# Order of the two gather streams of an expert mixer: V rows ahead of U rows in each pair, with small moves in opening, selection and end

## The chip, the cores and the metric

The kernel runs on one NeuronCore of a Trainium2 chip. The metric is device time in microseconds (us) of one execution. Engines are called by their short names: PE is TensorE, ACT is ScalarE, DVE is VectorE, POOL is GpSimd, SP is SyncE.

## The reference, cut to what matters

One layer of a decoder is computed for 256 prompt tokens and 8 sample tokens of width 2048. The first half (projections, gated linear attention, short convolution, output projection) is dense matmul work and takes the first 940 us. The second half is an expert mixer, and the change is mostly there:

```
ht = h.reshape(T, D)
q = (ht @ w_query).reshape(T, PEER_HEADS, 2, DQ_HALF)       # 8 heads, 2 halves
s1, s2 = scores of both halves against 128 keys each
v1, i1 = lax.top_k(s1, 16);  v2, i2 = lax.top_k(s2, 16)
top, pos = lax.top_k(v1[..., :, None] + v2[..., None, :], 16)   # of 256 candidates
idx = i1 * 128 + i2 at pos;  g = softmax(top)
u = expert_u[idx];  a = einsum('thkd,td->thk', u, xb)      # dot of each U row with the token
w = g * gelu(a)
y = x + einsum('thk,thkd->td', w, expert_v[idx])           # weighted sum of V rows
y = rmsnorm(y, norm_f_g)
```

For each token and head 16 rows of 8 KB are read from `expert_u`, and the same 16 from `expert_v`. The weight of a V row is known only when all 16 dots of that head and token are done.

## The kernel before, in words

**Blocks.** The 256 prompt tokens are two tiles of 128. A block `b` is one head of one tile: blocks 0 to 7 are the 8 heads of tile 0, blocks 8 to 15 those of tile 1. A block needs 16 gathers (`s` = 0 to 15) from `expert_u` and 16 from `expert_v`; one gather is one indirect DMA of POOL (L736) that brings 128 rows of 8 KB (1 MB) into one slot of a ring. The sample tokens add 8 U gathers in block 10 and 8 V gathers in block 12.

**U and V.** The U gathers of block `b` lie beside the V gathers of block `b-1`: the loop over `b` and `s` issues U(b, s) and then V(b-1, s). The U row set is consumed by DVE: `dot` (L1513) multiplies it with the tokens and sums. After the last dot of a block ACT applies Gelu (L1065), DVE scales with the softmax share and spreads the result (L1553, L1528), PE turns it (L1951), and DVE makes `weigher` of it (`turned_w`, L1546). DVE's program has `weights_of(b-1)` after dot(b, 0) and `turned_w(b-1)` after dot(b, 1). Only then PE may consume V(b-1, 0): `weigh` (L1970), 4 matmuls a gather that accumulate in a PSUM bank. In blocks 1 and 9 a `begin_sum` (L1958, 4 matmuls) goes ahead of the first `weigh` of each four.

**The ring.** `order_of` is the list of all gathers in order; gather n takes slot n % 6 up to n = 35 and then slot (n - 36) % 8. `free_slot` lets POOL wait until the gather that had the slot before is eaten: by DVE's count `u_used` or PE's count `pe_used`. POOL issues strictly in the order of the list, so one slot that isn't free holds up every gather behind it. Block 1 begins with gather 16, on a ring of 6; from its middle on the ring has 8.

**Beside it.** DVE also finds the experts of block b+1 during block b: `keys_of` after dot(b, 1), `pairs_of` after dot(b, 4), `experts_of` after dot(b, 7). PE makes the query projections of the heads 3 to 7 in blocks 1 to 3. SP loads `w_query` in pieces of 2 MB while the gathers run, and when the last query matmul is done (L581) it loads `gf_c`, the final norm's factors, spread over the partitions (L583).

**Opening.** The 256 prompt tokens are scaled with 1/rms in eight pieces of 512 columns: two by DVE (L1138), three by ACT (L795), three by POOL (L658). PE turns 16 column blocks (`turn(k)`, L1725), ACT and DVE split each into two parts (`act_hi` L799, `act_lo` L1148), and the small projection `rank_rows(g)` (L1738) is put between turns: g = 0 after turn 11, g = 1 after turn 14, g = 2 and 3 after all. Then `first_queries` (L1749) begins the dense part.

**Selection.** For block 0 the experts are found in two halves of eight (`first_experts`, L1443), so that the first gathers can go before the second half is known. POOL's first gather waits for the count `retrieved` (L1473).

**End.** Tile 1's outputs go out in four parts: ACT squares a bank (L1026), PE sums over partitions (L1996), DVE makes the mean (L1567), ACT the root (L1033), DVE the reciprocal (L1576) and the scaled result times `gf_c` (L1579), and SP stores it with four DMAs (L593).

## Time and profile before

| what | value |
|---|---|
| median of 3 runs (lowest, highest) | 2303.8 us (2303.49, 2305.24) |
| time of the profiled execution | 2304.25 us |
| its span | 2302.5 us |
| PE, DVE, ACT, POOL busy | 1586.5, 1318.1, 559.9, 731.2 us |
| DMA moved | 780.93 MB, mean 339 GB/s |
| of it by POOL's queue (the gathers) | 597.80 MB |
| issue to landing, median, U and V gathers | 17.0 and 17.3 us |

The table has averages over two very different halves. Up to about 940 us PE is busy nine tenths and more; after that the DMA engines are busy nine tenths and more. So a row of the whole span says little, and each stage has to be read for itself. The executions agree within 0.08%.

### The profile page before, as it was taken

How to read it: one execution, taken by the hardware profiler on the slowest of the kernel's cores; microseconds unless marked ns; L12 is line 12 of the kernel's file. 1: busy time of each engine (PE TensorE's matmuls, PEld its weight loads, DVE VectorE, ACT ScalarE, POOL GpSimd, SP SyncE). 2: the span in 40 equal slices, each digit the busy share in tenths (PEclk: the TensorE clock that was granted, in tenths of full speed). 3: DMA queues.
4: the chain of work that ended last, by engine and by line, in shares of the span. 5: the costliest groups of instructions: out<-in, count | busy, mean ns of one | idle time of the engine just before them, and what ended most of it. 6: DMA issues, size and time to landing. Idle time of an engine off the chain costs nothing.

```text
span 2302.5 us, 26069 instructions
## 1 busy us (share of the span) xinstructions
PE 1586.5 (69%) x10425; PEld 1088.1 (47%) x10425; DVE 1318.1 (57%) x2002; ACT 559.9 (24%) x775; POOL 731.2 (32%) x735
## 2 busy tenths in 40 slices
PE   9999999999999999957674334444343334434345
PEld 8999999999999999834341000000000000000001
DVE  6544556646555564675554665566566665465541
ACT  5333555545555544310000000000000000000000
POOL 1000110110111101444553444544345554344342
PEclk9999999999999999988885555555565555555556
DMA  8876878887878776799999999999999999999998
GB/s 243 224 192 197 237 227 240 247 247 211 256 209 252 220 227 211 292 417 427 423 427 392 388 427 427 427 428 427 427 422 427 427 427 427 428 427 423 427 414 349
DMA packets 435165, 780.93 MB, mean 339 GB/s; under 512 B 39640, under 2 KB 353904, under 8 KB 367200
## 3 DMA queue, kind: packets, MB, share of 16 engines
q0 software_dynamic: 89424, 597.80, 62.6%
q1 hardware_dynamic: 344000, 179.19, 28.1%
q10 hardware_dynamic: 1624, 2.31, 0.3%
q8 instruction: 82, 1.34, 0.2%
q14 instruction: 35, 0.29, 0.0%
HBM read 755.95 MB, written 23.35 MB: 338 GB/s over the span
## 4 chain that ended last, share of the span: by engine, by line
PE 45%; DMA 39%; DVE 6%; POOL 6%; issue 4%; ACT 1%; POOLq 0%; ACTq 0%; DVEq 0%
DMA ring<-in_expert_u,idx_all 27%; PE bank L1770 12%; PE bank L1771 12%; PE bank L1772 12%; DMA ring<-in_expert_v,idx_turned 10%; POOL ring L736 6%; DVE ring L1513 3%; PE bank L1970 3%; PE bank L1924 2%; DMA ring<-in_expert_v,idx_s 1%; DMA ring<-in_expert_u,idx_s 1%; PE bank L1880 1%; PE bank L1861 1%; DMA x2T<-x_turned 0%; DVE weigher L1546 0%
## 5 line engine op out<-in xcount | busy, mean ns | idle before, releaser
L1970 PE MATMUL bank<-ring,weigher 128*32 128x512 f32 x2048 | 450.1, 976 | 624.8 <-DMA ring<-in_expert_v,idx_turned 567.3
L1513 DVE CUSTOM_DVE_ANT_0 ring<-ring,xn_tok 128x2048 f32<-128x2048 f32 x256 | 585.8, 2291 | 477.0 <-DMA ring<-in_expert_u,idx_all 475.9
L1770 PE MATMUL bank<-act_hi,w_hi 128*128 128x264 f32 x2272 | 653.0, 287 | 0.3 <-DVE x2T L1369 0.3
L1771 PE MATMUL bank<-act_lo,w_hi 128*128 128x264 f32 x2272 | 643.8, 283 | 0.0
L1772 PE MATMUL bank<-act_hi,w_lo 128*128 128x264 f32 x2272 | 643.5, 283 | 0.0
L1110 DVE TENSOR_TENSOR w_lo<-raw,w_hi 128x2048 fp32r<-128x2048 f32 x142 | 325.6, 2293 | 321.3 <-ACT w_hi L771 320.6
L1970 PEld LDWEIGHTS bank<-ring,weigher 128*32 128x32 f32 x2048 | 53.0, 136 | 952.5 <-DMA ring<-in_expert_v,idx_turned 867.8
L736 POOL DMA_INDIRECT ring<-in_expert_u,idx_all x256 | 301.3, 1177 | 431.7 <-DVE w_all L1513 274.4
L1770 PEld LDWEIGHTS bank<-act_hi,w_hi 128*128 128x128 f32 x2272 | 427.9, 188 | 19.5 <-issue 19.1
L1771 PEld LDWEIGHTS bank<-act_lo,w_hi 128*128 128x128 f32 x2272 | 428.2, 188 | 1.7 <-issue 1.7
L1772 PEld LDWEIGHTS bank<-act_hi,w_lo 128*128 128x128 f32 x2272 | 426.0, 187 | 0.0
L736 POOL DMA_INDIRECT ring<-in_expert_v,idx_turned x256 | 305.1, 1192 | 324.4 <-PE bank L1970 257.5
L771 ACT ACTIVATE w_hi<-raw 128x2048 fp32r<-128x2048 f32 x142 | 272.1, 1916 | 417.3 <-PE bank L1772 413.4
L690 POOL DMA_DIRECT2D out<-s_ring x64 | 34.9, 545 | 496.6 <-DVE s_ring L1325 496.6
L1065 ACT ACTIVATE w_all<-w_all 128x16 f32<-128x16 f32 x16 | 3.5, 216 | 659.1 <-DVE w_all L1513 659.1
L1924 PE MATMUL bank<-h2T,wq 128*128 128x264 f32 x448 | 119.7, 429 | 0.0
L1924 PEld LDWEIGHTS bank<-h2T,wq 128*128 128x128 f32 x448 | 93.5, 213 | 38.2 <-issue 20.8
L1017 ACT ACTIVATE soft<-soft,rstd 128x16 f32<-128x16 f32 x16 | 4.9, 307 | 331.4 <-DVE soft L1418 331.3
L1951 PEld LDWEIGHTS bank<-div,widened 128*128 128x128 f32 x64 | 15.1, 293 | 110.3 <-issue 93.7
L1951 PE MATMUL bank<-div,widened 128*128 128x16 f32 x64 | 17.9, 359 | 63.7 <-DVE widened L1528 63.3
L664 POOL DMA_DIRECT2D v_samples<-v_tok x1 | 0.8, 754 | 163.4 <-DVE v_tok L1233 163.4
L998 ACT ACTIVATE q_s<-bank 128x8 f32<-128x8 f32 x16 | 2.8, 173 | 134.6 <-PE bank L1924 134.1
(318 smaller groups left out, 1183.2 us busy)
## 6 DMA issues: line engine op xcount, KB each, us to landing
raw<-in_w_in SPq DMA_DIRECT2D x129, 1024.0 KB, 6.8
s_ring<-in_state_gla POOLq DMA_DIRECT2D x64, 256.0 KB, 6.0
out<-s_ring POOLq DMA_DIRECT2D x64, 256.0 KB, 5.8
raw<-in_w_out SPq DMA_DIRECT2D x16, 1024.0 KB, 5.5
wq<-in_w_query SPq DMA_DIRECT2D x8, 2048.0 KB, 20.8
v_row<-v_samples POOLq DMA_DIRECT2D x32, 256.0 KB, 6.0
ring<-in_expert_u,idx_all POOLq DMA_INDIRECT x256, 17.0
ring<-in_expert_v,idx_turned POOLq DMA_INDIRECT x256, 17.3
```

Of the source, the lines that this page charges most:

```text
L690: g.dma_start(st_out[:, step // M, k, j, :], s_ring[step % N_S][:]).then_inc(s_out[step % N_S], 16)
L736: g.indirect_dma_start(ring[slot_of[n]][:], None, table, bass.IndirectOffsetOnAxis(ap=idx, axis=0)).then_inc(ring_in[slot_of[n]], 16)
L771: a.activation(w_hi[n0 % 2][:], raw[s][:], ACT.Copy).then_inc(hi_done, 1)
L1110: v.tensor_tensor(w_lo[n0 % 2][:], raw[s][:], w_hi[n0 % 2][:].bitcast(F32), ALU.subtract).then_inc(lo_done, 1)
L1513: v.tensor_tensor_reduce(ring[k][:], ring[k][:], xn_tok[:, b // PH, :], 1.0, 0.0, ALU.mult, ALU.add, w_all[:, b * TOPK + s:b * TOPK + s + ...
L1770: mm(out, hi_, act_hi[:, k, :], start=(k == 0), stop=False)
L1771: mm(out, hi_, act_lo[:, k, :], start=False, stop=False)
L1772: ins = mm(out, lo_, act_hi[:, k, :], start=False, stop=(k == KT - 1))
L1861: ins = mm(bank[KV0 + k][:], k_tok[:, k, :], v_, start=True, stop=True)
L1924: ins = mm(out, w[:, k, cols_], h2T[:, k, :], start=(k == 0), stop=(k == KT - 1))
L1951: mm(bank[z_bank(kind, b)][:, 0:TOPK], widened[n % 2][:].rearrange("p j k -> p (j k)"), div8[:], start=True, stop=True).then_inc(z_mm, 1)
L1970: ins = mm(bank[sum_bank(t, j)][c * STRIP:(c + 1) * STRIP, :], weigher[b % 2][:, s, :], ring[k][:, c * 512:(c + 1) * 512], start=False, st ...
```

## The change

It does five things.

1. `order_of` and POOL's loop: in each pair V(b-1, s) now comes ahead of U(b, s). The slots follow the list. POOL's wait for `retrieved` moves with the U gather. DVE's and PE's programs keep their order; only the slots that they name change.
2. Opening: the piece (part 3, tile 1) is scaled by DVE and no longer by ACT; `rank_rows(0)` goes after turn 13, `rank_rows(1)` after the last turn.
3. Selection of block 0: `match_replace` of the 256 candidates goes from ahead of the first `retrieved` to behind it; the cast of the first half's keys goes up between the two key searches.
4. End: for the last quarter of tile 1 the product with `gf_c` is made ahead of the mean, the scaling is split into 256 columns on DVE and 256 on ACT, and of the four stores SP issues two and ACT two.
5. Four matmuls of the identity (`warm`) go ahead of PE's wait for the last V gather.

```diff
@@ -62,6 +62,7 @@
     B_END = B_QRY + 2 * PH
     N_PAR = 6
     WARM = (16, 16, 4)
+    LAST_WARM = 4
     STRIP = 32
     N_CONSTS, N_LATE_CONSTS = 25, 12
     N_LINKS = 18
@@ -279,6 +280,7 @@
         ROWS = 4
         QUERIES = {1: (3, 4), 2: (5, 6), 3: (7,)}
 
+        LEFT, RIGHT = (slice(3 * 512 + x * 256, 3 * 512 + (x + 1) * 256) for x in range(2))
         TILE_0, SAMPLES = [(0, j) for j in range(4)], [(2, 0)]
         Y_ORDER = TILE_0 + SAMPLES + [(1, j) for j in range(4)]
 
@@ -296,10 +298,10 @@
         order_of = []
         for g in range(N_BLK + 1):
             for s in range(TOPK):
+                if g > 0:
+                    order_of.append((V_, g - 1, s, "pe"))
                 if g < N_BLK:
                     order_of.append((U_, g, s, "dot"))
-                if g > 0:
-                    order_of.append((V_, g - 1, s, "pe"))
                 if g == S_U and s % 2:
                     order_of.append((US_, 0, s // 2, "dot"))
                 if g == S_V and s % 2:
@@ -585,9 +587,9 @@
             yp = y_prompt.rearrange("b l d -> (b l) d")
             ys = y_sample.rearrange("b s d -> (b s) d")
             for nth, (t, j) in enumerate(Y_ORDER):
-                sp.wait_ge(y_ready, nth + 1)
+                sp.wait_ge(y_ready, nth + 1 if nth < N_SUM - 1 else N_SUM + 2)
                 rows = TS if t == 2 else STRIP
-                for c in range(4):
+                for c in range(4 if nth < N_SUM - 1 else 2):
                     row0 = 0 if t == 2 else t * P + j * STRIP
                     out = (ys if t == 2 else yp)[row0:row0 + rows, c * 512:(c + 1) * 512]
                     sp.dma_start(out, y_out_at[c * STRIP:c * STRIP + rows, t, j * 512:(j + 1) * 512]).then_inc(y_out, 16)
@@ -737,19 +739,21 @@
                                      bass.IndirectOffsetOnAxis(ap=idx, axis=0)).then_inc(ring_in[slot_of[n]], 16)
 
             for b in range(N_BLK + 1):
-                if b < N_BLK:
-                    pool.wait_ge(retrieved, b + 2 if b else 1)
                 if b == S_U:
                     pool.wait_ge(s_picked, 1)
                 for s in range(TOPK):
+                    if b > 0 and s == 0:
+                        pool.wait_ge(z_read, nth_z("idx", b - 1) + 1)
+                    if b > 0:
+                        fetch(ev, V_, b - 1, s, idx_turned[:, (b - 1) % 3, s:s + 1])
+                    if b == 0 and s == 0:
+                        pool.wait_ge(retrieved, 1)
                     if b == 0 and s == 8:
                         pool.wait_ge(retrieved, 2)
-                    if b == 1 and s == 0 or b > 1 and s == 0:
-                        pool.wait_ge(z_read, nth_z("idx", b - 1) + 1)
+                    if 0 < b < N_BLK and s == 0:
+                        pool.wait_ge(retrieved, b + 2)
                     if b < N_BLK:
                         fetch(eu, U_, b, s, idx_all[:, b * TOPK + s:b * TOPK + s + 1])
-                    if b > 0:
-                        fetch(ev, V_, b - 1, s, idx_turned[:, (b - 1) % 3, s:s + 1])
                     if b == S_U and s % 2:
                         fetch(eu, US_, 0, s // 2, idx_s[:, s // 2:s // 2 + 1])
                     if b == S_V and s % 2:
@@ -790,8 +794,8 @@
             act.wait_ge(par_T, 1)
             a.activation(pcol[:], bank[0][:, 0:120], ACT.Copy).then_inc(par_ready, 1)
             act.wait_ge(rs_done, 1)
-            for part, t in ((1, 0), (1, 1), (3, 1)):
-                cols_ = slice(part * 512, (part + 1) * 512)
+            for t in range(2):
+                cols_ = slice(512, 1024)
                 a.activation(x_tok[:, t, cols_], x_tok[:, t, cols_], ACT.Copy, scale=rstd[:, t:t + 1]).then_inc(xa_done, 1)
             act.wait_ge(par_ready, 1)
             for k in range(KT):
@@ -1091,6 +1095,13 @@
             for j in range(4):
                 y_squares([(1, j)])
                 y_roots(2 + j, [(1, j)])
+            act.wait_ge(y_ready, N_SUM)
+            act.wait_ge(y_rstd, 6)
+            a.activation(y_out_at[:, 1, RIGHT], y_out_at[:, 1, RIGHT], ACT.Copy, scale=y_rs[:, N_SUM - 1:N_SUM]).then_inc(y_ready, 1)
+            act.wait_ge(y_ready, N_SUM + 2)
+            for c in (2, 3):
+                act.dma_start(y_prompt.rearrange("b l d -> (b l) d")[P + 3 * STRIP:2 * P, c * 512:(c + 1) * 512],
+                              y_out_at[c * STRIP:(c + 1) * STRIP, 1, 3 * 512:4 * 512]).then_inc(y_out, 16)
 
 
 
@@ -1138,6 +1149,8 @@
                     v.tensor_scalar(x_tok[:, t, cols_], x_tok[:, t, cols_], rstd[:, t:t + 1], None,
                                     ALU.mult).then_inc(xn_done, 1)
                 v.tensor_scalar(xs_n[:], xs_flat[:], rstd[:, 2:3], None, ALU.mult).then_inc(xs_scaled, 1)
+                cols_ = slice(3 * 512, 4 * 512)
+                v.tensor_scalar(x_tok[:, 1, cols_], x_tok[:, 1, cols_], rstd[:, 1:2], None, ALU.mult).then_inc(xn_done, 1)
 
             def act_parts():
 
@@ -1407,6 +1420,8 @@
                     work = [(sc[:, 0, 0, s, :], val[:, s, :], key_u[:, s, :])]
                     top8(work, 0)
                     top8(work, 1)
+                    if s == 0:
+                        v.tensor_copy(key_f[:, 0, :], key_u[:, 0, :])
 
             def best_pairs(r, rows):
                 chained(v.tensor_tensor(cand[r, :].rearrange("p (a b) -> p a b", a=TOPK),
@@ -1443,8 +1458,7 @@
             def first_experts():
 
                 shape = [P, TS, TOPK]
-                for s in range(2):
-                    v.tensor_copy(key_f[:, s, :], key_u[:, s, :])
+                v.tensor_copy(key_f[:, 1, :], key_u[:, 1, :])
                 chained(v.tensor_tensor(cand[:].rearrange("p (a b) -> p a b", a=TOPK),
                                         val[:, 0, :].unsqueeze(2).broadcast_to([P, TOPK, TOPK]),
                                         val[:, 1, :].unsqueeze(1).broadcast_to([P, TOPK, TOPK]), ALU.add))
@@ -1452,8 +1466,6 @@
                     eight = slice(8 * turn, 8 * turn + 8)
                     chained(v.max(best[:, eight], cand[:]))
                     chained(v.max_index(pos[:, eight], best[:, eight], cand[:]))
-                    if turn == 0:
-                        v.match_replace(cand[:], best[:, eight], cand[:], NEG_BIG)
                     v.tensor_scalar(pos_u[:, 0, eight], pos[:, eight], 4, None, ALU.logical_shift_right)
                     chained(v.tensor_scalar(pos_u[:, 1, eight], pos[:, eight], 15, None, ALU.bitwise_and))
                     for s in range(2):
@@ -1472,6 +1484,8 @@
                     chained(ins)
                     v.scalar_tensor_tensor(out=idx_all[:, eight], in0=key_sel[:, 0, eight], scalar=float(NKEY),
                                            in1=key_sel[:, 1, eight], op0=ALU.mult, op1=ALU.add).then_inc(retrieved, 1)
+                    if turn == 0:
+                        chained(v.match_replace(cand[:], best[:, eight], cand[:], NEG_BIG))
                 v.tensor_tensor(soft[:], best[:], best[:, 0:1].broadcast_to([P, TOPK]), ALU.subtract).then_inc(soft_in, 1)
                 chained(v.scalar_tensor_tensor(out=idx_f[:], in0=key_sel[:, 0, :], scalar=float(NKEY),
                                                in1=key_sel[:, 1, :], op0=ALU.mult, op1=ALU.add))
@@ -1696,9 +1710,18 @@
                                 y_means(nth, parts)
                             if s == 6:
                                 y_scale(nth, parts)
-            for j in range(4):
+            for j in range(3):
                 y_means(2 + j, [(1, j)])
                 y_scale(2 + j, [(1, j)])
+            dve.wait_ge(y_ss, N_SUM)
+            v.tensor_tensor(y_out_at[:, 1, 3 * 512:4 * 512], bank[sum_bank(1, 3)][:], gf_c[:], ALU.mult).then_inc(y_ready, 1)
+            y_means(5, [(1, 3)])
+            dve.wait_ge(y_root, 6)
+            v.reciprocal(y_rs[:, N_SUM - 1:N_SUM], y_rt[:, N_SUM - 1:N_SUM]).then_inc(y_rstd, 1)
+            dve.wait_ge(y_rstd, 6)
+            dve.wait_ge(y_ready, N_SUM)
+            v.tensor_scalar(y_out_at[:, 1, LEFT], y_out_at[:, 1, LEFT], y_rs[:, N_SUM - 1:N_SUM], None,
+                            ALU.mult).then_inc(y_ready, 1)
 
 
 
@@ -1718,7 +1741,7 @@
                 if k == 8:
                     pe.wait_ge(xp_done, 2)
                 if k == 12:
-                    pe.wait_ge(xa_done, 3)
+                    pe.wait_ge(xn_done, 3)
                     pe.wait_ge(xp_done, 3)
                 b = bank[2 + k % 6]
                 for t in range(2):
@@ -1799,10 +1822,9 @@
                 if k == 2:
                     pe.wait_ge(xs_scaled, 1)
                     tr(bank[1][:, 2 * P:3 * P], xs_n[:], ident[:]).then_inc(xs_tr, 1)
-                if k == 11:
+                if k == 13:
                     rank_rows(0)
-                if k == 14:
-                    rank_rows(1)
+            rank_rows(1)
             rank_rows(2)
             rank_rows(3)
             pe.wait_ge(par_ready, 1)
@@ -1965,6 +1987,8 @@
                     pe.wait_ge(z_read, nth_z("w", b) + 1)
                 if b % PH == 0 and s % 4 == 0:
                     begin_sum(t, j)
+                if b == N_BLK - 1 and s == TOPK - 1:
+                    warm(LAST_WARM)
                 pe.wait_ge(ring_in[k], landed(V_, b, s))
                 for c in range(4):
                     ins = mm(bank[sum_bank(t, j)][c * STRIP:(c + 1) * STRIP, :], weigher[b % 2][:, s, :],
```

The order of the instructions shows what moves. POOL, the gathers from number 16 on (first pair of block 1; `ring_194` to `ring_199` are the six slots), before:

```order
L736 DMA ring_198<-in_expert_u,idx_all 128x2048 [waits u_used,z_read,retrieved]
L736 DMA ring_199<-in_expert_v,idx_turned 128x2048 [waits u_used]
L736 DMA ring_194<-in_expert_u,idx_all 128x2048 [waits u_used]
L736 DMA ring_195<-in_expert_v,idx_turned 128x2048 [waits u_used]
L736 DMA ring_196<-in_expert_u,idx_all 128x2048 [waits u_used]
L736 DMA ring_197<-in_expert_v,idx_turned 128x2048 [waits u_used]
L736 DMA ring_198<-in_expert_u,idx_all 128x2048 [waits u_used]
L736 DMA ring_199<-in_expert_v,idx_turned 128x2048 [waits pe_used]
```

and with the change:

```order
L738 DMA ring_198<-in_expert_v,idx_turned 128x2048 [waits u_used,z_read]
L738 DMA ring_199<-in_expert_u,idx_all 128x2048 [waits u_used,retrieved]
L738 DMA ring_194<-in_expert_v,idx_turned 128x2048 [waits u_used]
L738 DMA ring_195<-in_expert_u,idx_all 128x2048 [waits u_used]
L738 DMA ring_196<-in_expert_v,idx_turned 128x2048 [waits u_used]
L738 DMA ring_197<-in_expert_u,idx_all 128x2048 [waits u_used]
L738 DMA ring_198<-in_expert_v,idx_turned 128x2048 [waits pe_used]
L738 DMA ring_199<-in_expert_u,idx_all 128x2048 [waits u_used]
```

The first wait for PE (`pe_used`) comes one gather earlier, at gather 22 and not at 23, and a U gather now stands behind it.

PE in the opening, from turn 11 on (L1725 are turns, L1738 `rank_rows`), before:

```order
L1738 MATMUL bank<-act_hi,raw_69 32x264 [waits xs_lo,raw_in0,par_ready,al_done]
L1738 MATMUL bank<-act_hi,raw_69 32x264 x3
L1738 MATMUL bank<-act_lo,raw_69 32x264 x4
L1725 MATMUL bank<-ident,x_tok 128x128 [waits xp_done,xa_done,al_done]
L1725 MATMUL bank<-ident,x_tok 128x128
```

and with the change (L1748 are turns, L1761 `rank_rows`):

```order
L1748 MATMUL bank<-ident,x_tok 128x128 [waits xp_done,xn_done,al_done]
L1748 MATMUL bank<-ident,x_tok 128x128
L1748 MATMUL bank<-ident,x_tok 128x128 [waits al_done]
L1748 MATMUL bank<-ident,x_tok 128x128
L1761 MATMUL bank<-act_hi,raw_69 32x264 [waits xs_lo,raw_in0,par_ready,al_done]
```

The turns 12 and 13 stand ahead of the first `rank_rows`, and turn 12 waits for DVE's piece in place of ACT's.

## Rows read from the trace of the kernel before

**Rows 1.** The page's GB/s line: 40 equal slices of 57.6 us.
```profile
GB/s 243 224 192 197 237 227 240 247 247 211 256 209 252 220 227 211 292 417 427 423 427 392 388 427 427 427 428 427 427 422 427 427 427 427 428 427 423 427 414 349
```
**Rows 2.** Busy time by stretch; the last three columns are clock, DMA share, GB/s.
```profile
1220.00:1240.00 20.00, 6.34 (x26) 1.10 (x26) 8.10 (x7) 0.00 (x0) 7.51 (x9) 0.55 1.01 382
...
1300.00:1320.00 20.00, 8.28 (x34) 1.31 (x34) 13.58 (x27) 0.00 (x0) 10.76 (x8) 0.50 1.01 387
...
1340.00:1360.00 20.00, 8.09 (x34) 1.50 (x34) 12.86 (x27) 1.50 (x2) 7.82 (x7) 0.50 1.01 426
```
**Rows 3.** Timeline of SP at 1200 to 1230: start, us, engine, line, operation.
```profile
1214.58 1.74 SPq L583 DMA_DIRECT2D gf_c<-in_norm_f_g  x4
```
**Rows 4.** Timeline, beginning of block 5: [idle before <- what ended it].
```profile
1344.79 2.29 DVE L1513 CUSTOM_DVE_ANT_0 ring<-ring,xn_tok 128x2048 f32<-128x2048 f32 x1 [2.56 <-DMA ring<-in_expert_u,idx_all]
...
1349.74 2.29 DVE L1513 CUSTOM_DVE_ANT_0 ring<-ring,xn_tok 128x2048 f32<-128x2048 f32 x1 [2.24 <-DMA ring<-in_expert_u,idx_all]
...
1351.96 0.69 DVE L1546 TENSOR_TENSOR weigher<-bank,own 128x512 f32<-128x512 f32 x1
...
1352.70 3.64 PE L1970 MATMUL bank<-ring,weigher 128*32 128x512 f32 x16 [4.48 <-DVE weigher L1546]
1354.94 0.94 POOL L736 DMA_INDIRECT ring<-in_expert_v,idx_turned  x1 [6.63 <-PE bank L1970]
```
**Rows 5.** DMA issues at 950.5 to 951.5: the first gather, us from issue to landing.
```profile
ring<-in_expert_u,idx_all POOLq DMA_INDIRECT x1, 5.7
```
**Rows 6.** Timeline, beginning of block 1.
```profile
1013.78 0.94 POOL L736 DMA_INDIRECT ring<-in_expert_u,idx_all  x1 [0.31 <-issue]
1014.28 2.29 DVE L1513 CUSTOM_DVE_ANT_0 ring<-ring,xn_tok 128x2048 f32<-128x2048 f32 x1 [1.11 <-DMA ring<-in_expert_u,idx_all]
...
1017.24 1.94 PE L1958 MATMUL bank<-x_tok,ident 128*32 128x512 f32 x8 [3.34 <-DVE weigher L1546]
...
1021.00 2.29 DVE L1513 CUSTOM_DVE_ANT_0 ring<-ring,xn_tok 128x2048 f32<-128x2048 f32 x1 [0.94 <-DMA ring<-in_expert_u,idx_all]
1021.17 2.93 POOL L736 DMA_INDIRECT ring<-in_expert_v,idx_turned  x1 [6.45 <-PE bank L1970]
...
1030.61 1.07 PE L1970 MATMUL bank<-ring,weigher 128*32 128x512 f32 x8 [0.38 <-DMA ring<-in_expert_v,idx_turned]
```
**Rows 7.** Timeline: dot(9, 0), V(8, 4)'s issue; then dot(15, 0), V(14, 4)'s issue.
```profile
1661.05 2.29 DVE L1513 CUSTOM_DVE_ANT_0 ring<-ring,xn_tok 128x2048 f32<-128x2048 f32 x1 [2.59 <-DMA ring<-in_expert_u,idx_all]
...
1672.96 2.10 POOL L736 DMA_INDIRECT ring<-in_expert_v,idx_turned  x1 [8.38 <-PE bank L1970]
...
2178.46 2.29 DVE L1513 CUSTOM_DVE_ANT_0 ring<-ring,xn_tok 128x2048 f32<-128x2048 f32 x1 [2.57 <-DMA ring<-in_expert_u,idx_all]
...
2188.56 2.80 POOL L736 DMA_INDIRECT ring<-in_expert_v,idx_turned  x1 [6.57 <-PE bank L1970]
```
**Rows 8.** Timeline of the opening.
```profile
11.73 1.32 DVE L1138 TENSOR_SCALAR x_tok<-x_tok,rstd 128x512 f32<-128x512 f32 x2
...
12.19 1.94 ACT L795 ACTIVATE x_tok<-x_tok,rstd 128x512 f32<-128x512 f32 x3
...
20.21 1.21 ACT L799 ACTIVATE act_hi<-bank,pcol 128x256 fp32r<-128x256 f32 x3 [1.21 <-PE bank L1725]
...
24.13 0.40 PE L1749 MATMUL bank<-act_hi,w_hi 128*128 128x264 f32 x1
```
**Rows 9.** Timeline of DVE, selection of block 0.
```profile
947.83 0.09 DVE L1456 MATCH_VALUE_LOAD cand<-best,cand 128x8 f32 x1
947.91 0.41 DVE L1456 MATCH_REPLACE8 cand<-best,cand 128x256 f32<-128x256 f32 x1
```
**Rows 10.** Timeline of the end; then line L593: min, median, max in ns.
```profile
2297.69 0.16 DVE L1567 TENSOR_SCALAR y_ms<-bank 128x1 f32<-128x1 f32 x1 [3.46 <-PE bank L1996]
...
2298.32 0.75 DVE L1579 SCALAR_TENSOR_TENSOR x_tok<-bank,y_rs,gf_c 128x512 f32<-128x512 f32 x1
...
L593 SPq DMA_DIRECT2D out<-x_tok x36: 287/421/555, 1694.6 to 2300.4; - x36
```

## The prediction

> **What bounds the kernel now.** I read the page's slices first. From the eighteenth on, that is from about 980 us to 2290, the DMA engines move 417 to 428 GB/s in nearly every slice [rows 1]. A gather is 1,048,576 bytes, at 427 GB/s 2.45 us, and a pair 4.9. So the second half is a stream of gathers that runs without a hole, and DVE and PE follow it: the idle time ahead of dots and of V matmuls ends with a landing [rows 4]. Two slices stand out, 392 and 388. The table of stretches shows them as 100 us, from 1220 to 1320, in which five stretches of 20 us read 382 to 388 at a DMA share of 1.01; at 1340 it is 426 at the same share [rows 2]. The engines are as busy there, but slower. That stretch costs 100 x (1 - 386/427) = 9.6 us. No wait explains it. It begins within some us of SP's loads of `gf_c` at 1214.58 [rows 3]. All four executions known lie within 1.8 us of each other, so each of them had it.
>
> Hence an exchange of U and V in a stream that is always full gains nothing by itself. It can lose, by a hole, and it can change that stretch.
>
> **Part 1, the pairs: the beginning of a block.** Call A the landing of V(b-1, 0). Nothing may eat it until dot(b, 1) is done and `weigher` is made. In block 5 dot(5, 0) starts at 1344.79, with its landing; dot(5, 1) at 1349.74, `weigher` at 1351.96, PE at 1352.70, and POOL issues V(4, 4), which needs the slot of V(4, 0), at 1354.94: 10.15 us behind dot(5, 0) [rows 4]. Before, V(4, 0) lands behind U(5, 0), now 2.45 us ahead of it. So POOL's issue comes at A + 10.15 + 2.45 = A + 12.6. Eight slots hold the stream until A + 8 x 2.45 = A + 19.6, when V(b-1, 4) must have landed. The trace has one gather with an empty queue, the first: 5.7 us from issue to landing [rows 5]. A + 12.6 + 5.7 = A + 18.3: 1.3 us early. The blocks 2 to 8 and 10 to 14 (twelve) therefore cost nothing; the cover is those 1.3 us. In the steady part V and U alternate as before, and nothing changes.
>
> The Trainium skill (DMA: Bandwidth & Descriptors, Anatomy of one DMA) fits a POOL-issued DMA as about 2.0 us plus bytes over 436 GB/s, which would be 4.4 us for a gather; the row says 5.7, and the row decides. By the page each of the three costs below would be smaller by 1.3 us, or zero, and the sum 2.9 us lower; I name it because it speaks for an easier change than I count.
>
> Three blocks have less cover.
> - Block 1, ring of six. Before, gather 22 is U(1, 3) and goes at 1013.78; V(0, 3) waits for PE until 1021.17 [rows 6]. Now gather 22 is V(0, 3). U(1, 1) is gather 19 and no longer 18; as 18 landed at 1014.28 and 20 at 1021.00, 19 is put in the middle, 1017.6, 3.4 us later. `weigher`, `begin_sum` at 1017.24 and the freed slot shift with it: POOL issues at 1021.17 + 3.4 = 1024.6, it lands at 1030.3, gather 23 at 1032.7. Before, 23 was eaten from 1030.61 on [rows 6]. Cost +2.1 us. Bounds: 0, as SP's `w_query` load can fill the hole, and +3.4, the full shift of the release, if nothing of it is absorbed.
> - Block 9, where `begin_sum` goes ahead. POOL's issue is 11.91 us behind dot(9, 0) and takes 2.10 us in place of 0.94, since it falls into a dot [rows 7]. Landing A + 2.45 + 11.91 + 5.7 + 1.16 = A + 21.2, so +1.6 us; bounds 0 and 2.45 (a whole gather).
> - Block 15: 10.10 us behind the dot, and 2.80 us long [rows 7]. Landing A + 12.55 + 5.7 + 1.86 = A + 20.1: +0.5 us; same bounds.
>
> At the end of the stream U(15, 15) lands one gather later and V(15, 0) is weighed some 2.5 us later; PE needs 3.64 us for two [rows 4] where the stream needs 4.9, so it catches up within a few gathers. Nothing.
>
> **Part 2, opening.** ACT's three pieces take 1.94 us [rows 8], 0.65 each; one goes to DVE, where two take 1.32 and DVE would otherwise wait for ACT. ACT starts its split 0.65 us earlier, and the 1.21 us that it stands still at 20.21, behind `rank_rows(0)` [rows 8], shrinks. But PE then has three `rank_rows` in a row to do, so I take only the first, -0.65, by which `first_queries` leaves 24.13 [rows 8]; the dense part is PE's and carries it on. Bounds 0 and -1.9 (both).
>
> **Part 3, selection.** `match_replace`, 0.09 and 0.41 with overlap [rows 9], leaves the way to the first gather. -0.5 at most, 0 at least. I take 0: the stream starts earlier, but block 1's hole is timed by DVE and PE and gives it back.
>
> **Part 4, end.** The scaling of 0.75 us becomes two halves beside each other, about 0.4 by DVE's pieces [rows 8], but the product of 0.75 is on DVE when the mean would start at 2297.69 [rows 10], which delays it by 0.3. Together 0. Two of SP's four stores, 0.42 us each [rows 10], go to ACT: -0.85. Bounds 0 and -1.2. The skill says (same page, Issuing engines are not separate DMA queues) that a second issuing engine saves only the issue time; that is just what I count. The four `warm` matmuls lie in PE's wait for a landing: 0, hidden by the stream.
>
> **Sum.** 2.1 + 1.6 + 0.5 - 0.65 + 0 - 0.85 = +2.7 us on the profiled execution's 2304.25, so 2306.9, and 2306.4 on the scale of the median, which lies 0.45 lower. What a measurement can tell from no change is 0.2%, 4.6 us. The small terms alone stay within it. What decides is the slow stretch.
>
> **Forecast: the slow stretch is gone, or nearly.** Its cost of 9.6 us leaves: 2306.4 - 9.6 = 2296.8, rounded 2297. For it: nothing in the program asks for this stretch; the 40 slices show it once in 1300 us, though loads, stores and block starts come many times; and the change gives the gathers another order and another distance to everything beside them just where it begins. Against it: I have no mechanism, only a coincidence in time, and `gf_c` is loaded at the same place of the program. Chance 0.40.
>
> **Rival 1: the stretch stays as it is,** because the load, or the end of the query matmuls beside it, makes it. Then the sum stands, 2306, which is no change. For it: four executions with the same time, so it is no accident. Chance 0.37.
>
> **Rival 2: the ring runs dry at every block start, slower.** The place is POOL's issue of V(b-1, 4), the cover 1.3 us. An issue that falls into a dot takes up to 2.80 us [rows 7], 1.86 more than usual. If that happens in the twelve blocks too, each lands at A + 12.6 + 5.7 + 1.86 = A + 20.2 and costs 0.55 us, together 6.6, and with the stretch in place the time is 2313. It decides as soon as issue and delay together pass A + 13.9. Against it: in block 5 the issue takes 0.94 [rows 4], as DVE is then at its small key operations and starts the next dot only behind them. A slow stretch that begins as before and lasts half as long again (+4.8, 2311) ends on the same side; both have 0.23. That the change doesn't do what it says is excluded by the order of the instructions.
>
> **How the numbers follow.** Faster by over 0.2%: 0.41 (the forecast, and a little of a stretch that is shortened). Within 0.2%: 0.36. Slower: 0.23. The range goes from 2292 (forecast with block 1, 9 and 15 at 0 and the opening at its better bound) to 2313 (rival 2). The forecast's own range is 2292 to 2300.
>
> **What would show it.** Slices of 427 GB/s where 392 and 388 stood: forecast; 387 from some point behind L585 on: rival 1. The wait of POOL for PE at block starts 2.45 us longer, 9.1 where 6.63 stood. A gap between dots of block 1 of 2 us more. The first `first_queries` matmul at 23.5. Two stores by ACT, and the time from the last V landing to the end 0.85 us shorter. DMA shares below 1.0 in a 20 us stretch at the start of blocks 2 to 14 would be rival 2. The forecast is wrong if the stretches of 387 together are longer than 50 us.

## The result, and the profile after

The changed kernel takes 2307.19 us (median of 20 executions, 2303.2 to 2337.1), the kernel before 2296.09 in the same comparison (20 executions, 2293.99 to 2305.74). The ratio is 1.0053 with a 95% interval of 1.0037 to 1.0069: slower by about half a per cent. The forecast was 2297, faster. It is wrong, in sign and in size.

The spread must be read with the medians. The kernel before has two groups of times: 12 of the 20 lie from 2294.0 to 2297.8, and 8 from 2303.5 to 2305.7. The three times known ahead of the prediction and the profiled execution (2304.25) belonged to the upper group. At its share in all executions of that kernel (36 of 125, below) four of four would come by pure chance about 7 times in a thousand, so why they did is open. Of the changed kernel, 8 of 20 lie from 2303.2 to 2304.3, and the others are spread up to 2337. So there are two questions: why the lowest times are 8 to 9 us apart, and what makes the long ones. The profiled execution after took 2328.71 us (span 2327.0) and shows both. Its slices, to be held against [rows 1]:

```profile
PEclk9999999999999999978885555555555555555556
DMA  9877877887878776899999999999999999999998
GB/s 251 224 191 200 241 228 237 245 236 222 240 230 255 209 225 220 328 379 426 423 412 376 377 376 410 424 421 419 428 402 427 428 424 427 427 425 423 428 412 351
```

Before, from the eighteenth slice on nearly all read 422 to 428, but for one dip. Now 376 and 377 stand in three slices in a row, and others read 379, 412, 410 and 402. The table of stretches (the last three columns are clock, DMA share and GB/s) shows the first kind:

```profile
1220.00:1240.00 20.00, 6.92 (x34) 1.27 (x34) 11.29 (x26) 0.00 (x0) 7.81 (x8) 0.56 1.02 373
1240.00:1320.00 80.00, 26.93 (x118) 3.70 (x114) 42.77 (x77) 3.09 (x4) 39.71 (x29) 0.52 1.01 377
1320.00:1400.00 80.00, 26.88 (x116) 4.15 (x116) 45.33 (x61) 3.09 (x4) 40.74 (x29) 0.52 1.01 376
...
1415.00:1420.00 5.00, 1.94 (x8) 0.20 (x8) 2.20 (x3) 0.00 (x0) 1.42 (x3) 0.50 1.03 415
1420.00:1500.00 80.00, 36.81 (x140) 7.40 (x140) 48.07 (x81) 5.26 (x8) 39.20 (x33) 0.54 1.01 425
```

It is the slow stretch of [rows 2], at the same place: the DMA engines are full (share 1.01) and move 376 GB/s in place of 427. It lasts 195 us here and 100 before, and costs 195 x (1 - 376/427) = 23 us of this execution's 25 above the lowest time.

The second kind is a stream that runs dry. The timeline at the beginning of block 1, to be held against [rows 6] (L738 is the gather, L1527 the dot, L1560 `weigher`, L1980 `begin_sum`, L1994 the V matmuls, L1946 the query matmuls):

```profile
1010.77 2.29 DVE L1527 CUSTOM_DVE_ANT_0 ring<-ring,xn_tok 128x2048 f32<-128x2048 f32 x1 [1.02 <-DMA ring<-in_expert_u,idx_all]
1010.86 3.01 POOL L738 DMA_INDIRECT ring<-in_expert_u,idx_all  x1 [0.30 <-issue]
1016.35 2.29 DVE L1527 CUSTOM_DVE_ANT_0 ring<-ring,xn_tok 128x2048 f32<-128x2048 f32 x1 [2.78 <-DMA ring<-in_expert_u,idx_all]
1018.56 0.69 DVE L1560 TENSOR_TENSOR weigher<-bank,own 128x512 f32<-128x512 f32 x1
...
1019.31 1.93 PE L1980 MATMUL bank<-x_tok,ident 128*32 128x512 f32 x8 [5.01 <-DVE weigher L1560]
1021.01 1.93 PE L1994 MATMUL bank<-ring,weigher 128*32 128x512 f32 x8
...
1023.15 2.29 DVE L1527 CUSTOM_DVE_ANT_0 ring<-ring,xn_tok 128x2048 f32<-128x2048 f32 x1 [1.02 <-DMA ring<-in_expert_u,idx_all]
1023.25 3.01 POOL L738 DMA_INDIRECT ring<-in_expert_v,idx_turned  x1 [9.37 <-PE bank L1994]
...
1033.57 2.29 DVE L1527 CUSTOM_DVE_ANT_0 ring<-ring,xn_tok 128x2048 f32<-128x2048 f32 x1 [8.12 <-DMA ring<-in_expert_u,idx_all]
```

POOL waits 9.37 us for PE where it waited 6.45, issues V(0, 3) at 1023.25, and DVE then stands idle 8.12 us until U(1, 3) lands. At the beginning of block 5 the same wait, 12.81 us, ends at 1369.70 (before 6.63 [rows 4]); that is inside the slow stretch, so the kernel with the pairs alone, below, is the cleaner comparison.

The opening and the end, to be held against [rows 8] and [rows 10]:

```profile
12.38 1.33 ACT L799 ACTIVATE x_tok<-x_tok,rstd 128x512 f32<-128x512 f32 x2
...
13.36 0.82 DVE L1153 TENSOR_SCALAR x_tok<-x_tok,rstd 128x512 f32<-128x512 f32 x1
...
22.98 0.39 PE L1772 MATMUL bank<-act_hi,w_hi 128*128 128x264 f32 x1
...
949.05 1.04 POOL L738 DMA_INDIRECT ring<-in_expert_u,idx_all  x1 [79.40 <-DVE idx_all L1485]
...
2315.66 1.93 PE L1994 MATMUL bank<-ring,weigher 128*32 128x512 f32 x8
...
2317.53 2.08 PE L1780 MATMUL bank<-ident 128*128 128x128 f32 x8
...
2319.53 1.94 PE L1994 MATMUL bank<-ring,weigher 128*32 128x512 f32 x8
2321.53 0.60 ACT L1030 ACTIVATE y_junk<-bank 128x512 f32<-128x512 f32 x1 [5.37 <-PE bank L1994]
...
2324.08 0.85 ACTq L1103 DMA_DIRECT2D out<-x_tok  x2
```

`first_queries` leaves at 22.98 in place of 24.13, and the first gather at 949.05 in place of 950.80, so opening and selection give 1.75 us to the start of the stream. From the last sum of squares to the end it takes 5.5 us (2321.53 to 2327.0) against 6.0 before (2296.53 to 2302.5). But the four warming matmuls take 2.08 us and stand ahead of the last V: 3.87 us from the start of V(15, 14) to the start of V(15, 15), 2.44 before. Nor do they warm anything here: the last V takes 1.94 us at a granted clock of 0.50, where it took 1.07 at 1.00 before.

### The profile page after: what moved, and what is told of

The parts are those of the page before. It is cut to its first block, busy times and chain, and to the rows that moved or that the text cites. A ratio compares the mean times of both kernels' runs of the same rounds, so it can differ in the third digit from the quotient of the medians.

```text
span 2327.0 us, 26102 instructions
## 1 busy us (share of the span) xinstructions
PE 1575.7 (68%) x10433; PEld 1093.3 (47%) x10433; DVE 1320.1 (57%) x2004; ACT 560.3 (24%) x775; POOL 782.5 (34%) x735
## 3 DMA queue, kind: packets, MB, share of 16 engines
q10 hardware_dynamic: 1720, 2.44, 0.3%
q8 instruction: 82, 1.34, 0.2%
## 4 chain that ended last, share of the span: by engine, by line
PE 45%; DMA 36%; POOL 8%; DVE 6%; issue 4%; ACT 0%; POOLq 0%; ACTq 0%; DVEq 0%
DMA ring<-in_expert_u,idx_all 26%; PE bank L1793 12%; PE bank L1794 12%; PE bank L1795 12%; DMA ring<-in_expert_v,idx_turned 9%; POOL ring L738 8%; DVE ring L1527 4%; PE bank L1994 3%; PE bank L1946 2%; DMA ring<-in_expert_v,idx_s 1%; PE bank L1902 1%; PE bank L1883 1%; DMA x2T<-x_turned 0%; DVE weigher L1560 0%; PE bank L1780 0%
## 5 line engine op out<-in xcount | busy, mean ns | idle before, releaser
L1527 DVE CUSTOM_DVE_ANT_0 ring<-ring,xn_tok 128x2048 f32<-128x2048 f32 x256 | 586.0, 2292 | 520.6 <-DMA ring<-in_expert_u,idx_all 520.0
L1994 PE MATMUL bank<-ring,weigher 128*32 128x512 f32 x2048 | 435.9, 956 | 568.5 <-DMA ring<-in_expert_v,idx_turned 507.8
L1994 PEld LDWEIGHTS bank<-ring,weigher 128*32 128x32 f32 x2048 | 56.2, 138 | 877.8 <-DMA ring<-in_expert_v,idx_turned 768.7
L738 POOL DMA_INDIRECT ring<-in_expert_v,idx_turned x256 | 337.1, 1317 | 361.7 <-PE bank L1994 298.5
L738 POOL DMA_INDIRECT ring<-in_expert_u,idx_all x256 | 322.0, 1258 | 370.3 <-DVE w_all L1527 200.2
L1946 PE MATMUL bank<-h2T,wq 128*128 128x264 f32 x448 | 119.6, 428 | 0.0
L1946 PEld LDWEIGHTS bank<-h2T,wq 128*128 128x128 f32 x448 | 93.4, 213 | 38.1 <-issue 20.7
L677 POOL DMA_DIRECT2D s_ring<-in_state_gla x64 | 34.5, 541 | 3.2 <-issue 2.5
```

What stands on the lines that cost most here:

```text
L677: g.dma_start(s_ring[n % N_S][:], st_in[:, n // M, k, j, :]).then_inc(s_in[n % N_S], 16)
L738: g.indirect_dma_start(ring[slot_of[n]][:], None, table, bass.IndirectOffsetOnAxis(ap=idx, axis=0)).then_inc(ring_in[slot_of[n]], 16)
L1527: v.tensor_tensor_reduce(ring[k][:], ring[k][:], xn_tok[:, b // PH, :], 1.0, 0.0, ALU.mult, ALU.add, w_all[:, b * TOPK + s:b * TOPK + s + ...
L1946: ins = mm(out, w[:, k, cols_], h2T[:, k, :], start=(k == 0), stop=(k == KT - 1))
L1994: ins = mm(bank[sum_bank(t, j)][c * STRIP:(c + 1) * STRIP, :], weigher[b % 2][:, s, :], ring[k][:, c * 512:(c + 1) * 512], start=False, st ...
```

## The experiments

Each kernel ran 12 times, in three groups of four kernels, each group beside 35 executions of the kernel before. Times are given as lowest, median and highest, since single executions lie up to 34 us above the lowest of the same kernel. A ratio is to the kernel before.

**Theory 1:** with V first, the first V row of a block is held some 2.45 us longer before it can be eaten, the ring is short of a slot, and the gather stream runs dry at block starts. Its rival: the small moves cost the time.

**The order of the pairs alone** (the kernel before, with only this):

```diff
-                if g < N_BLK:
-                    order_of.append((U_, g, s, "dot"))
                 if g > 0:
                     order_of.append((V_, g - 1, s, "pe"))
+                if g < N_BLK:
+                    order_of.append((U_, g, s, "dot"))
```
(and POOL's loop to match)

> The kernel before with the pair order alone (V of the older block ahead of U of the newer), opening, selection and end as they were. Undisturbed executions of before take 2294 to 2296 us, of the change 2303.2 to 2304.3. Theory 1 (holes in the gather stream at the starts of blocks 1, 9 and 15 cost the 8.4 us): this kernel's lowest times are 2301.5 to 2303.5, and the profile shows the hole of some 4.5 us in block 1. Theory 2 (the small moves cost it, by the warming matmuls or by a later start of the stream): its lowest times are 2294 to 2297. Whether the stretch of slow packets shows (10 us each) is left to chance by both.

Measured: 2303.3, 2306.3, 2315.6; ratio 1.0038 (1.0020 to 1.0056). The order of the pairs carries the whole loss: 8.9 us at the lowest time (2294.4 for the kernel before in this group).

**The small moves alone** (the change, with the pairs as they were before).

> The change with the pair order undone: the small moves in opening, selection and end alone. Theory 1: the lowest times are 2293.5 to 2296 (opening -0.7 to -1.2, end -0.5, warming matmuls ahead of the last V +1.5 to +2), no hole in block 1. Theory 2: 2301 to 2304. If also here times of 2310 and more are found, a stretch of slow packets that lasts longer than in before has nothing to do with the order of the pairs.

Measured: 2291.8, 2293.7, 2301.4; ratio 0.9978 (0.9960 to 0.9996). The small moves gain about 2 us when U stays first, more than either theory had expected. With V first nothing of that is left: the lowest time of the pairs alone is 2303.3, that of the whole change 2303.2.

**No warming:**

```diff
-                if b == N_BLK - 1 and s == TOPK - 1:
-                    warm(LAST_WARM)
```

> The change without the four warming matmuls ahead of the last V matmuls. If they delay the last V (profile: they run 2.08 us from 2317.53 on and the last V takes 1.94 us behind them, against 1.07 before), the lowest times are 1 to 2 us below the change's, 2301.5 to 2302.5. If they raise the clock for what follows, or lie in a wait, 2303.4 or more.

Measured: 2302.4, 2305.0, 2312.9; ratio 1.0032 (1.0016 to 1.0049); 0.8 us lower than the change at the lowest time. In its profile the last V starts 2.30 us behind the one before it, in place of 3.87, and takes the same 1.93:

```profile
2290.89 1.93 PE L1992 MATMUL bank<-ring,weigher 128*32 128x512 f32 x8
...
2293.19 1.93 PE L1992 MATMUL bank<-ring,weigher 128*32 128x512 f32 x8 [0.37 <-DMA ring<-in_expert_v,idx_turned]
```

That is 1.57 us in the two profiles. In the five other profiled kernels with the warming the clock has risen behind it, and the last V takes 1.06 to 1.21 us; without it, it takes 1.93 or 1.94 in seven profiled kernels, this one among them, and 1.07 in the kernel before. From the start of V(15, 14) to the end of the last V it is 4.7 us with the warming and 4.4 without, with U first, and 5.1 and 4.4 with V first and the early weigher (below). There the warming costs 0.3 and 0.7 us, and between the change and this kernel 1.6.

**Block 1 with U first** (all others V first; `g > 1` and `g == 1` in the two lists).

> The change, with U ahead of V in the pairs of block 1 alone, so that U(1, 1) is gather 18 again and V(0, 3) gather 23. Theory 1: the hole in block 1 (4.5 us of an idle DMA side) closes, the lowest times are 2298 to 2299.5, 4 to 5 us below the change's; the holes at blocks 9 and 15 (1.7 and 0.9 us) stay. Rival (the hole is filled by other work and the loss lies spread over all block starts): 2302.5 or more.

Measured: 2298.35, 2303.4, 2317.7; ratio 1.0024 (1.0004 to 1.0044). The lowest time is 4.9 us below the change's: as expected, block 1's hole is about 5 us of the 8. That is the lowest time and two near it (2298.5, 2299.7) of a kernel with a wide spread, so I take it as a size, not as a figure to a tenth.

**The weigher earlier.** If the late release is the cause, it can be taken away without changing the order of the gathers:

```diff
                             weights_of(b - 1)
+                            turned_w(b - 1)
...
-                        if s == 1:
-                            turned_w(b - 1)
```

Here `turned_w` stands ahead of dot(b, 1), where DVE was idle, and no longer behind it.

> The change, with the weigher made ahead of dot(b, 1): the first V of each block can be eaten some 3.7 us earlier (DVE stands idle from 1343.87 to 1346.09 there, and PE has the turned weights at 1344.6), so POOL issues V(b-1, 4) 2.7 to 3.7 us earlier. Theory 1 (the loss is the late release of the first V's slot at the block starts): most of the 8 us come back, lowest times 2295 to 2297, and the lost rate at the starts of blocks 2 to 14 is gone. Rival (V ahead of U is slower for another reason, the order of the transfers or POOL's issues inside dots): 2301 or more.

Measured: 2293.3, 2294.3, 2316.1; ratio 0.9996 (0.9975 to 1.0016). Ten of twelve lie from 2293.3 to 2295.9. The loss is gone, 9.9 us at the lowest time, more than expected. The profile shows the step, block 5, first with the pairs alone:

```profile
1341.15 2.29 DVE L1515 CUSTOM_DVE_ANT_0 ring<-ring,xn_tok 128x2048 f32<-128x2048 f32 x1 [2.57 <-DMA ring<-in_expert_u,idx_all]
...
1348.31 0.68 DVE L1548 TENSOR_TENSOR weigher<-bank,own 128x512 f32<-128x512 f32 x1
...
1351.29 0.94 POOL L736 DMA_INDIRECT ring<-in_expert_v,idx_turned  x1 [11.49 <-PE bank L1972]
```

and with V first and the early weigher:

```profile
1336.05 2.29 DVE L1527 CUSTOM_DVE_ANT_0 ring<-ring,xn_tok 128x2048 f32<-128x2048 f32 x1 [2.57 <-DMA ring<-in_expert_u,idx_all]
...
1339.52 0.69 DVE L1560 TENSOR_TENSOR weigher<-bank,own 128x512 f32<-128x512 f32 x1 [0.76 <-PE bank L1972]
...
1342.51 1.58 POOL L738 DMA_INDIRECT ring<-in_expert_v,idx_turned  x1 [7.82 <-PE bank L1993]
```

POOL's issue is 10.14 us behind the dot in the first and 6.46 in the second. The stretches at the block starts (1, 3, 9, 14 and 15), pairs alone:

```profile
1020.00:1030.00 10.00, 10.00 (x54) 4.97 (x47) 4.46 (x15) 0.00 (x0) 4.40 (x4) 0.84 0.87 321
1190.00:1210.00 20.00, 19.30 (x104) 10.96 (x96) 13.96 (x29) 0.65 (x3) 13.42 (x9) 0.90 0.98 386
...
1670.00:1680.00 10.00, 5.53 (x42) 1.28 (x34) 3.65 (x6) 1.49 (x2) 8.30 (x6) 0.84 0.85 306
2110.00:2120.00 10.00, 2.13 (x16) 0.16 (x8) 4.78 (x5) 0.00 (x0) 8.48 (x6) 0.77 0.99 378
2190.00:2200.00 10.00, 3.45 (x20) 0.36 (x12) 3.78 (x3) 0.00 (x0) 7.87 (x8) 0.67 0.91 350
```

and with the early weigher:

```profile
1020.00:1030.00 10.00, 9.83 (x59) 5.49 (x57) 4.44 (x8) 0.00 (x0) 5.52 (x6) 1.00 1.02 409
1190.00:1210.00 20.00, 16.70 (x81) 9.80 (x74) 11.96 (x18) 0.64 (x3) 16.44 (x11) 0.84 1.01 426
...
1670.00:1680.00 10.00, 3.87 (x16) 0.40 (x16) 7.31 (x16) 3.08 (x4) 4.68 (x5) 0.50 1.01 425
2110.00:2120.00 10.00, 3.87 (x16) 0.40 (x16) 7.56 (x15) 1.59 (x2) 5.99 (x6) 0.50 1.02 428
2190.00:2200.00 10.00, 3.87 (x16) 0.40 (x16) 4.79 (x5) 0.00 (x0) 3.75 (x5) 0.50 1.01 426
```

Neither of the two executions has a slow stretch, so the starts of the dots tell how the loss is spread: from dot(b, 0) to dot(b + 1, 0) (for block 15 to the last dot), what the kernels with V first and the late weigher take more than this one. Four of their profiled executions have no slow stretch:

```
us more, blocks          1    2 and 3   4 to 8    9   10 to 14   15    sum
pairs alone             2.5     1.9      0.3     1.8     0.5     1.3   8.3
no warming              2.9     2.3      1.5     1.8    -1.2     1.2   8.5
no gf_c load (below)    2.3     1.7      1.8     1.9    -0.8     1.5   8.5
gf_c load later (below) 4.3     0.7      3.4     2.1    -0.4     0.7  10.8
```

The change itself takes 4.3 us more in block 1 too, ahead of its slow stretch. In these five profiles 4.3 and 2.3 to 2.9 are parted by a race. In the change and in the kernel of the last row POOL's issue of V(0, 3) begins 0.10 and 0.12 us behind the start of a dot and takes 3.01 and 2.99 us. In the other three it begins between 0.27 us ahead of a dot and 0.02 behind it, and takes 0.93 or 0.94. The load held back, then the pairs alone:

```profile
1022.90 2.99 POOL L739 DMA_INDIRECT ring<-in_expert_v,idx_turned  x1 [9.38 <-PE bank L1995]
...
1023.39 0.93 POOL L736 DMA_INDIRECT ring<-in_expert_v,idx_turned  x1 [9.45 <-PE bank L1972]
```

**U first with the early weigher, no warming.**

> Small moves without the warming matmuls, U ahead of V as in before, and the weigher of the older block made ahead of dot(b, 1) instead of behind it. The small moves with U ahead of V took 2293.5 typically (lowest 2291.8), the warming costs 1.0. With U first the stream has little left to win (0.4 to 1.5 us at the starts of blocks 14 and 15), so theory 1 expects 2291 to 2292.5 typically. Rival (DVE's wait for the turned weights now delays dot(b, 1) and so POOL): 2294 or more.

Measured: 2291.6, 2293.9, 2307.2; ratio 0.9982 (0.9963 to 1.0002). The median lies above the 2291 to 2292.5 expected and just under the rival's 2294, and the kernel is not told apart from the small moves alone (0.9978). With U first no hole is seen that it could close.

**The small moves without warming, U first.**

> The small moves alone (U first, weigher where it was) without the warming matmuls. With them: median 2293.7, lowest 2291.8. If the warming costs here what it costs with V first (1.0 us between the lowest times), the median is 2292.7 and the lowest 2290.8. If with U first the last V lands later than the warming ends, 2293.7.

Measured: 2292.3, 2294.2, 2303.0; ratio 0.9987 (0.9973 to 1.0002). The expectation was 1 us too low: no gain is seen with U first, as fits the 0.3 us that the warming costs there by the profiles. Between kernels of different groups half a microsecond can't be told.

**Now the slow stretch.** Theory A: the load of `gf_c`, 64 KB four times in 2 KB packets between the gathers, can leave the stream in a slow rate. Theory B: the end of the query matmuls beside it, or nothing in the program, does.

```diff
-            for c in range(4):
-                sp.dma_start(gf_c[c * STRIP:(c + 1) * STRIP, :], ...).then_inc(row_in, 16)
...
+                        v.memset(gf_c[:], 1.0)
```

> The change without the load of norm_f_g to gf_c: DVE fills gf_c with ones in block 5 instead, so the factor norm_f_g is left out of the outputs. Theory A (the load of gf_c, 256 packets on SP's queue between the gathers, brings the gathers into the slow rate of 352 ns a packet): no run above the floor, all within 2303 to 2305. Theory B (the end of the query matmuls, or chance, brings it): times are spread as the change's, half of them above 2305 and some above 2310.

Measured: 2302.0, 2304.3, 2306.6; ratio 1.0027 (1.0014 to 1.0040). Four of twelve are above the 2305 that theory A allowed, by up to 1.6 us; none is where theory B wanted some, above 2310. (The load is 128 packets of 2 KB in the DMA records, not 256.)

> The kernel before without the load of gf_c; DVE fills gf_c with ones in block 5, so the factor norm_f_g is left out of the outputs. The kernel before has 26 of 90 executions above 2302. Theory A: all twelve within 2294 to 2298. Theory B: three or four of twelve at 2303 to 2309.

Measured: 2292.8, 2294.3, 2295.7; ratio 0.9984 (0.9974 to 0.9995). Its lowest time is 1.6 us below that of the kernel before, and the upper group is gone, as theory A has it.

I call an execution long if it is 6.5 us or more above its kernel's lowest; I chose that limit after seeing the times. With the load, in all kernels of this document, 62 of 265 are long (the kernel before 36 of 125, the change 8 of 20). Without it, 0 of 24. At a share of 62 in 265 that would come by chance about twice in a thousand times. The profiles of the two kernels without the load have no slow stretch either. So the load is needed for the stretch, as far as such counts can show it. It doesn't suffice, since three of four executions with it are not long. What remains without the load, a spread of 4.6 us with V first (2302.0 to 2306.6), is more than the 2.9 us with U first (2292.8 to 2295.7): holes vary too, as the race in block 1 shows.

**The load later:** `sp.wait_ge(u_used, 7 * TOPK + 1)` ahead of it.

> The change with the load of gf_c held back to dot(7, 0), some 280 us later. Theory A: the slow rate begins there (about 1505 us) and not at 1220, and its length runs to one of the next 16 KB instruction fetches, 55, 125 or 190 us later in place of 20, 100 or 180, so times at 2303.5, 2308 to 2310, 2316. Theory B: it begins at 1220 as before.

Measured: 2303.6, 2305.4, 2311.6; ratio 1.0033 (1.0020 to 1.0047). One of twelve is long (2311.6), the profiled one isn't, so it does not show where a stretch would begin. Inconclusive.

**The load earlier**, in the kernel with U first and the early weigher:

```diff
-        gf_c = sb_at("gf_c", [P, 512], F32, at_raw)
+        gf_c = sb_at("gf_c", [P, 512], F32, at_raw + two)
...
-            sp.wait_ge(mm_done, B_END)
+            sp.wait_ge(mm_done, B_QRY + 12)
```

> Small moves without warming, U first, weigher ahead of dot(b, 1), and the load of gf_c sent as soon as the buffer of the query weights of head 5 is free (in block 2, about 1135 us, in place of 1215), in another place of SBUF. Theory A (the load can bring the gathers into the slow rate wherever it falls): 2291.6 to 2295 as without this move, with one or two of twelve above 2299, and a slow stretch, where there is one, begins at about 1140. Theory B (the place at 1215 matters, where the queries end): no run above 2297.

Measured: 2291.8, 2294.1, 2311.8; ratio 0.9986 (0.9967 to 1.0005). The load goes at 1134.5, and one execution of twelve is 20 us long: that is against theory B's "no run above 2297". The profiled execution is not the long one, so it is not shown that the 20 us are a slow stretch.

**The same with V first** (and no warming):

> The change with V first, the weigher ahead of dot(b, 1), no warming, and gf_c loaded at about 1135. V first with the early weigher took 2294.3 (lowest 2293.3) with the warming, so 2292.3 to 2293.5. If it is below the kernel with U first of the same call by over 1 us, V first is worth something once its hole is closed; theory 1 expects them equal within 1 us.

Measured: 2292.3, 2294.1, 2296.6; ratio 0.9986 (0.9974 to 0.9998). The medians of the two orders are equal (2294.06 and 2294.09), the lowest times 0.5 us apart. Once its hole is closed, V first costs and gains nothing that these times can show. This kernel and the small moves alone are faster than the kernel before by 0.1 to 0.2% and can't be told from each other. That all twelve of this one are short says little at a share of a quarter (3 in 100).

The three kernels with the load moved, taken together, say more. Of their 36 executions 2 are long, and of the 229 with the load at about 1215 60 are. If the place made no difference, so few would come about 6 times in a thousand. So the place of the load, or what runs beside it there, seems to matter as well: that the load is needed doesn't exclude that the end of the query matmuls or the last loads of `w_query` are needed too. No run tests this apart.

## Why the prediction was wrong

**"That stretch costs 9.6 us", "each of them had it", and so "the slow stretch is gone": the step that failed.** Size and place were right, its standing wasn't. Four executions within 1.8 us were taken as proof that every execution has it. Only 36 of 125 are in the upper group. The forecast took 9.6 us off 2306.4, a level at which most executions of the kernel before do not lie. Nor did the change take the stretch away: its profiled execution has it for 195 us, and 8 of 20 are long. "I have no mechanism, only a coincidence in time" was the right warning: without the load named there it isn't seen, and the change leaves the load where it was.

A second step failed with it: the holes, put at 4.2 us (2.1 + 1.6 + 0.5), cost 8.3 to 10.8. Had the first step alone failed, the lowest times would lie some 3 us above those of the kernel before (the sum of 2.7), and not 9.2 (2303.2 against 2294.0).

**Rival 1 (2306) had the right number for the wrong reason.** It is 2306.4 from a time with a stretch in it; measured is 2307.2, a median with 8 us of holes and, in 8 of 20, a stretch.

**The beginning of a block.** The mechanism is as written: the slot of V(b-1, 0) comes free at the dot + 10.14 (10.15 forecast), now 2.45 us later against the stream. POOL's wait there is 11.49 us, 9.1 forecast; the forecast left out that the issue before it is now that of U(5, 3), one gather earlier.
- Block 1: +2.1 forecast, 2.3 to 4.3 measured by dots, or 4.9 by undoing it alone, over the bound of 3.4. In the change the issue came at 1023.25, earlier than the 1024.6 forecast. But the term left out that this issue can fall into a dot, here that of 1023.15, and then takes 3.01 us in place of 0.94, though just this was counted for blocks 9 and 15. With these 2.1 us the term would be 4.2. The Trainium skill (SBUF — State Buffer, SBUF: two separate sides) says that a DVE operation with two inputs in SBUF and a GpSimd operation that reads SBUF lock a port that both need, and that the one that comes second is blocked. The trace agrees: begun 0.09 and 0.10 us behind a dot's start, the issues at 1010.86 and 1023.25 took 3.01 (an issue reads its row numbers from SBUF). The other way round it is not seen: of issues that began 0.11 and 0.27 us ahead of a dot (pairs alone, no gf_c load) the issue took 0.93 and 0.94 and the dot its usual 2.29.
- Block 9: +1.6 forecast, 1.8 to 2.1 measured. Block 15: +0.5 forecast, 0.7 to 1.5 measured, which is within its bounds of 0 and 2.45.
- "The blocks 2 to 8 and 10 to 14 therefore cost nothing; the cover is those 1.3 us": they cost 2.6 to 3.7 together, 0.7 to 2.3 of it in blocks 2 and 3. The step counted V(b-1, 4) alone. In block 3 of the pairs alone the loss is one gather later:

```profile
1189.19 1.94 PE L1972 MATMUL bank<-ring,weigher 128*32 128x512 f32 x8 [4.46 <-DVE weigher L1548]
...
1191.06 5.17 PE L1926 MATMUL bank<-h2T,wq 128*128 128x264 f32 x16
1191.67 0.94 POOL L736 DMA_INDIRECT ring<-in_expert_v,idx_turned  x1 [10.72 <-PE bank L1972]
...
1192.91 2.25 POOL L736 DMA_INDIRECT ring<-in_expert_u,idx_all  x1 [0.30 <-issue]
...
1197.77 1.39 POOL L736 DMA_INDIRECT ring<-in_expert_v,idx_turned  x1 [2.61 <-PE bank L1972]
```

  PE eats V(2, 0) and then has 5.17 us of query matmuls ahead of V(2, 1), so POOL waits another 2.61 us for the next slot. Blocks 1 to 3 have queries, which the prediction did not put into the sum. The rest of the twelve blocks I have not followed.

Rival 2 (ring dry at every block start, 2313) is thereby half right: right place and sign, dry in some of the blocks, 8.3 to 10.8 us in all with blocks 1, 9 and 15.

**Opening, selection.** -0.65 forecast, -1.15 measured at `first_queries`; selection 0 forecast, about -0.6 more by the first gather (1.75 in all). "Block 1's hole is timed by DVE and PE and gives it back" fits the lowest times with V first (2303.3 without the small moves, 2303.2 with, the warming included); with U first the small moves keep 2.6 us.

**End.** -0.85 forecast, -0.5 measured. **`warm`: "hidden by the stream" is wrong with V first:** 0.8 us at the lowest time, 1.6 by the profiles, as the last V lands while the warming runs.

Two sums of the prediction are off without changing anything: with a landing 1.3 us shorter the three costs fall by 3.1 us together and not by 2.9, and the low end of the range comes to 2291.4 and not 2292.

## What to carry to other kernels

Look at a few dozen times, or at least at two profiles, before you take a feature of one profile out of the sum; four equal times can be four draws from the upper group. When the order of two streams in one ring is exchanged, follow the buffer that is released last at each block's edge, for several gathers and through every other job of the engine that releases it. A step of 0.7 us done in an idle gap ahead of a long operation rather than behind it was worth 9.9 us with V first, all that the order had cost, and nothing that was seen with U first. And where an issue begins within 0.3 us of an operation that can block it, expect the same kernel to have two costs there.

## What the runs showed of the hardware

The stream of gathers has two rates. The DMA records of three profiled executions show it for 8 KB packets, as the median (outside the first 6 us most lie within 10 ns of it):

```
kernel                 slow from..to    packet (normal 309 ns)   16 KB packet of the instruction queue
before                 1224..1321       342 ns                   1321.1 (one at 1240.0 passed)
the change             1224..1416       352 ns                   1416.1 (1242.6 and 1327.0 passed)
block 1 with U first   1222..1323       352 ns                   1322.4 (one at 1238.9 passed)
```

In each, the packets are disturbed while the 2 KB packets of `gf_c` run, and then stay slow. Of an execution without a stretch they are back at 309 ns within some 6 us. The slow rate ends in all three within 1 to 2 us of the start of a 16 KB packet on the queue that the profile's page calls instruction (82 of them in an execution, 1.34 MB), which comes about every 80 us there. But four such packets passed inside the stretches and ended nothing, so such a packet doesn't suffice. If only these packets end it, a stretch has a length of 20, 100 or 180 us, and at 12% that costs 2, 12 or 22 us; the times in the upper part are spread more evenly than that. The block 1 kernel's stretch in the view by stretches:

```profile
1220.00:1225.00 5.00, 1.05 (x8) 0.20 (x8) 3.40 (x9) 0.00 (x0) 1.24 (x2) 0.50 1.01 371
...
1300.00:1320.00 20.00, 7.32 (x32) 0.81 (x32) 13.95 (x27) 0.00 (x0) 7.37 (x7) 0.50 1.02 376
1320.00:1330.00 10.00, 4.11 (x22) 0.90 (x18) 4.84 (x5) 0.00 (x0) 6.86 (x5) 0.50 1.01 411
1330.00:1340.00 10.00, 4.14 (x20) 0.40 (x16) 6.93 (x6) 0.00 (x0) 7.56 (x4) 0.50 1.01 426
```

That the load is needed is shown by the counts of the two kernels without it. That the instruction packet ends the stretch is a coincidence seen three times against four packets that ended nothing, and what differs between the two rates (the phase of the engines against each other would be a guess) is open.
